# A two-layer encoder with eight experts: one step of the wide expert moved in front of the sixth step of the first pass

## The reference

```python
def swiglu(h, w_gate, w_up, w_down):
    return (jax.nn.silu(h @ w_gate) * (h @ w_up)) @ w_down

def moe_swiglu(h, router_w, w_gate, w_up, w_down):
    logits = (h @ router_w).astype(jnp.float32)
    top_val, top_idx = lax.top_k(logits, TOP_K)          # TOP_K = 2
    top_w = jax.nn.softmax(top_val, axis=-1)
    gates = jnp.sum(jax.nn.one_hot(top_idx, N_EXPERTS) * top_w[..., None], axis=-2)
    y = jnp.zeros_like(h)
    for e in range(N_EXPERTS):                            # hidden width 3584
        y = y + gates[..., e:e + 1] * swiglu(h, w_gate[e], w_up[e], w_down[e])
    return y
```

## Time and profile before

| | us |
|---|---|
| runs | 1842.13, 1845.21, 1846.84, median 1845.21 |
| profiled execution | 1842.24, span 1840.5 |
| from the mark of (0,1) to that of W2 | 801.6 to 1086.0 |
| PE, DVE, ACT busy, share of the span | 93%, 75%, 59% |

### The profile page before, as it was taken

The page is one execution under the profiler, slowest core; times in us unless marked ns, Lnnn a source line. Parts: engine busy times, 40 slices in busy tenths (PEclk is TensorE's granted clock), DMA queues, the critical chain, the costliest instruction groups (busy, mean ns, idle before and its releaser), DMA issues. The chain is left out here.

```text
span 1840.5 us, 25922 instructions
## 1 busy us (share of the span) xinstructions
PE 1714.3 (93%) x9974; PEld 1384.8 (75%) x9974; DVE 1374.1 (75%) x1237; ACT 1090.9 (59%) x1082; POOL 50.7 (3%) x100
## 2 busy tenths in 40 slices
PE   4998998899999998989899999999999999999996
PEld 2997898789999885666676776767677766788784
DVE  5657457667767588479679878897988788898885
ACT  1444444453333355477677577777767778767674
POOL 2000000001101000000000000000000000000000
PEclk9998999999999999989899999999999999999998
DMA  9975277048888531269879898988999899999993
GB/s 302 340 256 178 92 253 251 4 157 311 292 289 284 196 100 62 69 252 385 300 276 339 319 346 317 385 324 316 363 351 362 288 347 359 389 346 338 361 347 106
DMA packets 245324, 503.84 MB, mean 274 GB/s; under 512 B 11328, under 2 KB 83168, under 8 KB 245216
## 3 DMA queue, kind: packets, MB, share of 16 engines
q1 hardware_dynamic: 230480, 458.78, 69.8%
q0 software_dynamic: 12032, 43.00, 6.3%
q10 hardware_dynamic: 2704, 0.60, 0.2%
HBM read 501.29 MB, written 1.05 MB: 273 GB/s over the span
## 5 line engine op out<-in xcount | busy, mean ns | idle before, releaser
L1438 DVE TENSOR_TENSOR wlo<-raw,whi 128x2048 fp32r<-128x2048 f32 x428 | 968.5, 2288 | 311.1 <-ACT whi L572 310.2
L572 ACT ACTIVATE whi<-raw 128x2048 fp32r<-128x2048 f32 x428 | 807.1, 1909 | 215.3 <-PE ps L895 85.5
L1259 PE MATMUL ps<-whi,ahi 128*128 128x512 f32 x896 | 299.5, 411 | 14.7 <-ACT whi L572 8.5
L1263 PE MATMUL ps<-wlo,ahi 128*64 128x512 f32 (+1 forms) x896 | 260.9, 398 | 16.6 <-DVE wlo L1438 16.6
L891 PE MATMUL ps<-ahi,whi 128*128 128x256 f32 x816 | 231.9, 284 | 1.7 <-DVE alo L1497 1.7
L895 PE MATMUL ps<-alo,whi 128*128 128x256 f32 x816 | 230.9, 283 | 0.0
L898 PE MATMUL ps<-ahi,wlo 128*128 128x256 f32 x816 | 230.9, 283 | 0.0
L1259 PEld LDWEIGHTS ps<-whi,ahi 128*128 128x128 f32 x896 | 167.3, 192 | 60.8 <-issue 24.3
L1263 PEld LDWEIGHTS ps<-wlo,ahi 128*64 128x64 f32 (+1 forms) x896 | 137.8, 156 | 90.7 <-DVE wlo L1438 28.4
L891 PEld LDWEIGHTS ps<-ahi,whi 128*128 128x128 f32 x816 | 156.1, 191 | 2.9 <-issue 2.3
L1259 PE MATMUL ps<-whi,alo 128*128 128x512 f32 x448 | 156.6, 390 | 0.0
(11 more groups left out here) (244 smaller groups left out, 2089.4 us busy)
## 6 DMA issues: line engine op xcount, KB each, us to landing
raw<-l_exp_w_gate SPq DMA_DIRECT2D x112, 1024.0 KB, 7.1
raw<-l_exp_w_up SPq DMA_DIRECT2D x112, 1024.0 KB, 7.9
raw<-l_exp_w_down SPq DMA_DIRECT2D x112, 1024.0 KB, 7.1
raw<-l_w_in SPq DMA_DIRECT2D x42, 1024.0 KB, 5.2
mraw<-mod_w POOLq DMA_DIRECT2D x80, 512.0 KB, 5.5
raw<-l_ffn_w_gate SPq DMA_DIRECT2D x14, 1024.0 KB, 5.1
raw<-l_ffn_w_up SPq DMA_DIRECT2D x14, 1024.0 KB, 6.3
raw<-l_ffn_w_down SPq DMA_DIRECT2D x14, 1024.0 KB, 6.5
```

The costliest lines, as they stand in the source:

```text
L572: act.activation(whi[s % SPL][:, :], raw[s % RAW][:, :], ACT.Copy).then_inc(hi_done, 1)
L1259: ins = pe.matmul(dst, stat, whi[s % SPL][:, a:a + BANK], start=start, stop=False, skip_group_check=True)
L1263: ins = pe.matmul(dst, stat, wlo[s % SPL][:, a:a + BANK], start=False, stop=stop, skip_group_check=True)
L1438: dve.tensor_tensor(wlo[s % SPL][:, :], raw[s % RAW][:, :], whi[s % SPL][:, :].bitcast(F32), ALU.subtract).then_inc(lo_done, 1)
```

## The change

A table, `WIDE_BEFORE`, names the steps in front of which the seven wide steps stand. W0 now stands in front of (0,5) instead of behind (0,6), W1 in front of (2,0) instead of (2,4); W2 to W6 keep their places. The sequence is (0,0) to (0,4), W0, (0,5), (0,6), W1, (2,0) to (2,6), W2, and on as before. With it move: the wide place's slot matrices from the aside of (0,3) to that of (0,2); its gather from (0,5) to (0,3), with the low parts in (0,4); the turning of place 0's gates from (0,4) to (0,6); the gather of place 2 from W0 to W1. No instruction is added or taken away.

```diff
@@ -85,15 +85,16 @@
+WIDE_BEFORE = ((0, 5), (2, 0), (3, 0), (3, 4), (4, 0), (4, 4), (5, 0))
+
 def sequence():
-    steps = [(0, i) for i in range(NF)]
-    wide = 0
-    for q in range(WIDE + 1, FIRST_M):
+    steps = []
+    for q in (0,) + tuple(range(WIDE + 1, FIRST_M)):
         for i in range(NF):
-            if i in (0, 4) and wide < NF:
-                steps.append((WIDE, wide))
-                wide += 1
+            if (q, i) in WIDE_BEFORE:
+                steps.append((WIDE, WIDE_BEFORE.index((q, i))))
             steps.append((q, i))
     return steps + [(FIRST_M, 0)]
...
+def scattered_before(n):
+    return sum(WIDE < u < FIRST_M and k == 3 for u, k in SEQ[:n])
+
+def gathered_in(i):
+    u, k = WIDE_BEFORE[i]
+    return u if k == 0 else None
...
-                if i == 5 and q == 0:
+                if i == 3 and q == 0:
                     aside = lambda: evacuate_gathers(WIDE, 4)
-                elif i % 2 == 0 and q == WIDE:
-                    early = lambda: evacuate_gathers(WIDE + 1 + i // 2, 6)
+                elif q == WIDE and gathered_in(i):
+                    early = lambda: evacuate_gathers(gathered_in(i), 6)
...
-                    pe.wait_ge(y_add, 1 + 4 * ((i + 1) // 2))
+                    pe.wait_ge(y_add, 1 + 4 * scattered_before(n))
...
             def gather_next(q, p=0):
-                if q == 0:
-                    pe.wait_ge(selT_e, 1)
-                else:
+                if q:
                     pe.wait_ge(y_add, 4 * (q - 1 + p) + 1)
...
-                    return {4: lambda: turn_gates(0, 6), 5: lambda: gather_next(0)}.get(i)
+                    return {3: lambda: gather_next(0), 6: lambda: turn_gates(0, 6)}.get(i)
...
-                (0, 2): routing_places,
-                (0, 3): lambda: (choose_gates(0), choose_slots(WIDE)),
-                (0, 4): lambda: turned_gates(0),
+                (0, 2): lambda: (routing_places(), choose_slots(WIDE)),
+                (0, 3): lambda: choose_gates(0),
+                (0, 4): lambda: (gathered_low(WIDE), choose_slots(WIDE + 1)),
                 (0, 5): lambda: diagonals(3),
-                (0, 6): lambda: (gathered_low(WIDE), choose_slots(WIDE + 1)),
-                **{(WIDE, 2 * k): lambda k=k: gathered_low(WIDE + 1 + k) for k in range(4)},
+                (0, 6): lambda: turned_gates(0),
+                **{(WIDE, i): lambda i=i: gathered_low(gathered_in(i)) for i in range(NF) if gathered_in(i)},
                 (WIDE + 1, 0): lambda: choose_gates(WIDE),
                 (WIDE + 1, 1): lambda: (turned_gates(WIDE), routing_spill()),
                 (WIDE + 1, 4): routing_extra,
```

More of the change, by code:

```diff
@@ L1376, in gather_next, with gather_after @@
             def gather_next(q, p=0):
-                if q == 0:
-                    pe.wait_ge(selT_e, 1)
-                else:
+                if q:
                     pe.wait_ge(y_add, 4 * (q - 1 + p) + 1)
                 gather(q + 1, 2 if PASSES[q] == "M" else 4, p)
-            def gather_after(i):
-                pe.wait_ge(selT_e, WIDE + 1 + i // 2 if i else 1)
-                gather(WIDE + 1 + i // 2, 6)
+            def gather_after(u):
+                pe.wait_ge(selT_e, u if u > WIDE + 1 else 1)
+                gather(u, 6)
             def middle_of(q, i, p=0, final=False):
                 if q == 0:
-                    return {4: lambda: turn_gates(0, 6), 5: lambda: gather_next(0)}.get(i)
+                    return {3: lambda: gather_next(0), 6: lambda: turn_gates(0, 6)}.get(i)
                 if q == WIDE:
-                    return (lambda: gather_after(i)) if i % 2 == 0 else None
+                    return (lambda: gather_after(gathered_in(i))) if gathered_in(i) else None
                 if (q, i) == (WIDE + 1, 1):
```

## The result

The changed kernel takes 1850.49 us, median of 7 runs (1849.33 to 1854.55), the kernel before 1844.4 us, median of 7 runs in the same comparison (1842.13 to 1846.84). The ratio is 1.0037, with a 95% interval of 1.0027 to 1.0047: 0.37% slower, and the medians differ by 6.1 us. The profiled execution took 1850.49 us with a span of 1848.8, against 1842.24 and 1840.5 before.

What follows compares the result with a forecast made beforehand. PE bounds the whole, with time lost where it waits or its clock is halved. The terms +8.8 + 0.7 - 1.3 - 4.3 + 3.1 + 0.1 = +7.1 us, against the median 1845.21, gave 1852 us, range 1844 to 1859.

Steps and rivals of the forecast that it cites:

- 1.: Gather moved from (0,5) to (0,3): same wait and clock fall, (0,3) and (0,4) take 28.1 + 19.5 us, no change.
- 2. and 3.: (0,5) and (0,6) take 21.8 + 16.3 us, +8.8; W0 21.4 and W1 25.1 us, nil.
- 4.: Wide place's slot matrices in (0,2), where DVE is waited for: +0.7 us; place 0's turned gates in (0,6): nil.
- 5.: (2,3) no longer stands ahead of a wide step: 16.1 us, less 1.3.
- 6.: (2,4) loses its place behind a wide step: 17.9 us, less 4.3, with a new wait of about 4.6 us.
- 7.: (2,5): the clock falls behind the new wait of 4.6 us: 16.6 us, plus 3.1.
- 8.: (2,6): DVE sets the pace after seven narrow steps in a row: +0.1 us, at most +0.7.
- no second fall: Clock stays at 2.4 GHz through (2,5): +4.0 us, 1849; chance 0.22.
- DVE's lead lasts: W1's rest carries over to (2,4), so `routing_extra` stays hidden: -2.0 us, 1843; chance 0.10.
- the gather without a stall: In (0,3) the gather does not stall PE, its wait and clock fall go: -5.6 us, 1839.6; chance 0.06.
- the fourth rival: More waits in the run of seven narrow steps, bound by DMAs: up to +13.4 us, 1858; chance 0.15.

## Why the prediction was right

I forecast 1852 us, in a range of 1844 to 1859, and a sum of +7.1 us. The median is 1850.49, the medians differ by 6.1, the stage of the profiled executions by 4.6, 289.0 us where I had 291.5. By its own steps:

1. The gather takes the same wherever it stands. The wait was 5.77 us again, 5.78 before. Its fall was shorter, (0,3) and (0,4) took 27.8 + 16.6 where I had 28.1 + 19.5, so the stage is 3.2 us better than the sum here. This one profile is no sign of a merit of the change: in other profiles with the changed order the same stretch took 28.0 + 18.6 us (wait filled) and 30.8 + 18.7 (`routing_extra` covered, second profile), and in one with the order of before (0,5) and (0,6) took only 28.2 + 16.5 (`routing_extra` uncovered). How long the clock stays down differs between executions. Whether the short fall is more frequent in one order is not shown; it would explain why the orders were equal with both asides covered and not with the waits filled.
2. and 3. The two narrow steps behind W0 took 21.8 + 15.8 (forecast 21.8 + 16.3), W0 and W1 21.5 and 25.1: right. The prediction named the cover of `diagonals`, behind W0. That the low parts also have one, ahead of W0, came with the window taken for (0,4) and was not named: luck of the arrangement. The gather moved alone put both asides into a plain narrow run, where they cost 0.29%.
4. Slot matrices in (0,2): 17.7, forecast 17.7.
5. (2,3): 16.0, forecast 16.1.
6. (2,4): 18.5, forecast 17.9, with the wait at 4.11 us, forecast 4.6. DVE was busy for 17.91 us, as forecast; the rest is that the clock had fallen before the mark, and the first four products behind the wait took 1.97 us, where behind the filled wait they took 1.14. This was the main step, and it is shown from three sides: the wait goes when `routing_extra` is covered, a like one comes without any move of a wide step when it is uncovered, and the like wait behind `routing_spill` goes in either order when that is covered.
7. (2,5): 17.4, forecast 16.6. The fall was longer than that in (2,2); that it comes from PE standing idle is shown by filling the wait.
8. (2,6): 16.2, forecast 16.4.

The rule of the Trainium skill that gaps of TensorE bring back the half clock (page "TensorE: Matmul & The Clock Gate", section "Why this matters for your kernels") agrees with the traces here: with the wait of 4.11 us empty the granted clock of (2,5) was 0.77, with it filled 1.00. The advice of the Trainium skill to interleave regimes (page "Perfetto Trace Analysis", section "Optimization Strategy") brought no gain here. Runs of 5, 2 and 7 narrow steps against 7, 4 and 3 cost 1.5 us in (2,6) with all waits filled, and 3.1 with only the two asides covered.

Of the rivals, "no second fall" would have come true with the wait filled only. "DVE's lead lasts" fell, as (2,4) shows, and the gather without a stall fell with the wait of 5.77 us. The DMA limit of the fourth rival is real, but with `routing_extra` in (2,4) it did not show, (2,6) at 16.2 us; it appeared only when this was moved away. What is still open is why covering `routing_extra` in the changed kernel gained 3.3 to 4.4 us by its ratios, where the stage of its first profile gained 6.5. A part is the DMA-bound (2,6), 1.2 to 2.6 us, and (3,0), 0.7 us. The rest can't be told from two profiles of one kernel that differ by 12.7 us in all: 5.4 of them before the stage, where nothing was changed, 5.0 behind the gather, 1.4 in (2,6).

## What to carry to other kernels

Where two engines share a pipeline with a few buffers, small chores of the second engine are nearly free behind a step that the first one bounds (`routing_extra`, 4.0 us of work, cost 0.4 to 0.7 us there), and cost their full length in a step that the second bounds. When such steps are reordered, look at which chores lose their cover, not only at the steps. In this kernel a wait of the matrix engine costs twice, once itself and once by the halved clock behind it, and products of zeros put into the wait save the second part. A change that moves cover from one chore to another is best followed by placing the chores anew: here that was worth 4 us in the order of before and 11 to 12 in the changed one, where the order itself, with the moves of the first pass, cost 2.0 us in the stage.

## What the runs showed of the hardware

TensorE's clock fell to its lower level behind waits of 3.6 us at the end of (0,1), and of 3.8, 3.9, 4.1 and 5.8 us, in every profile that had them empty, and in none where they were filled with products of zeros: those count as work. It fell behind shorter waits too. In (5,5) PE waits 2.75 us, in most profiles with a second wait of 1.07 soon after, and the clock fell in all ten profiles in which that was not filled; with the gather moved alone it fell behind 1.92 us. But behind 2.19 us there, and behind 2.36 us in (0,2) with all waits filled in the changed order, it did not fall. So the length of a wait alone does not tell. The first row is of the kernel before, the others of the changed kernel, where the fold behind them took 3.51 us:

```profile
817.65 1.15 PE L1263 MATMUL ps<-wlo,ahi 128*64 128x512 f32 x4 [3.57 <-DVE wlo L1438]
...
1553.53 1.17 PE L1271 MATMUL ps<-whi,ahi 128*128 128x512 f32 x4 [2.75 <-ACT whi L584]
1555.77 1.97 PE L1275 MATMUL ps<-wlo,ahi 128*64 128x512 f32 x4 [1.06 <-DVE wlo L1448]
1557.53 3.51 PE L1303 MATMUL ps<-arena 128*128 128x64 f32 x16
```

The same wait was followed by a fall of differing length from one execution to the next. Behind the gather's 5.8 us the two steps lost, by the share missing, 0.12 x 27.8 = 3.3 us in the changed kernel, 6.9 in the kernel before, and 0.17 x 30.8 + 0.16 x 18.7 = 8.2 with `routing_extra` covered, second profile. In the changed kernel the step behind `routing_extra` lost 0.23 x 17.4 = 4.0 us, the one behind `routing_spill` 0.17 x 18.2 = 3.1 us. The DMA engines gave 393 to 396 GB/s at most in these stretches.
